# A product-key expert mixer: h in PSUM, two banks for the sums, more gathered rows beside the dot products

## What is computed

```python
q = (tb @ wq).reshape(PEER_BLOCK, PEER_HEADS, 2, PEER_QDIM // 2)
s = jnp.einsum('thcd,hcnd->thcn', q, keys)            # 2 x 128 scores a head
...                                                    # 16 best pairs a head: e, g
a = jax.nn.gelu(jnp.einsum('td,thkd->thk', tb, u_tab[e]), approximate=False)
return jnp.einsum('thk,thkd->td', (g * a), v_tab[e])
```

## Time and profile before

| | us |
|---|---|
| median of 3 runs (4033.55 to 4056.06) | 4041.88 |
| the profiled execution | 4036.62 |
| its span | 4034.8 |
| expert stage, first to last matmul | 2018.2 to 3948.3 |

### The profile page before, as it was taken

The page is one execution under the profiler, slowest core; times in us unless marked ns, Lnnn a source line. Parts: engine busy times, 40 slices in busy tenths (PEclk is TensorE's granted clock), DMA queues, the critical chain, the costliest instruction groups (busy, mean ns, idle before and its releaser), DMA issues. The chain is left out here.

```text
span 4034.8 us, 59078 instructions
## 1 busy us (share of the span) xinstructions
PE 3311.0 (82%) x20585; PEld 2890.3 (72%) x20585; DVE 2778.2 (69%) x5881; ACT 1357.6 (34%) x3190; POOL 1709.0 (42%) x1341
## 2 busy tenths in 40 slices
PE   6999688566686892666589999999999999999994
PEld 3677455211376792555489999999999999999993
DVE  3223676100231199999779998999999889999885
ACT  3010466000221111887633333333333333333331
POOL 1010000000212441888765665665565565565560
PEclk7999799777788996776699999999999999999997
DMA  6632546999422331787598998998988988898983
GB/s 232 221 124 74 172 148 212 357 412 406 161 72 77 99 115 42 200 240 205 141 329 318 330 325 303 326 331 311 326 319 314 334 316 314 320 322 307 328 300 148
DMA packets 389552, 1001.89 MB, mean 248 GB/s; under 512 B 187044, under 2 KB 232975, under 8 KB 325688
## 3 DMA queue, kind: packets, MB, share of 16 engines
q1 hardware_dynamic: 323768, 491.18, 35.9%
q0 software_dynamic: 62656, 469.86, 32.2%
q10 hardware_dynamic: 2944, 38.77, 2.6%
HBM read 914.75 MB, written 152.04 MB: 264 GB/s over the span
## 5 line engine op out<-in xcount | busy, mean ns | idle before, releaser
L2174 DVE CUSTOM_DVE_ANT_0 e_uv<-e_uv,e_h 128x1024 f32<-128x1024 f32 x416 | 721.7, 1735 | 73.8 <-DMA e_uv<-peer_uv,k_g_idx 73.1
L2243 POOL DMA_INDIRECT e_uv<-peer_uv,k_g_idx x416 | 521.1, 1253 | 540.4 <-DVE e_pY L2186 496.8
L1475 PE MATMUL e_po<-e_ph,e_vh 128*128 128x320 f32 x2048 | 646.3, 316 | 59.2 <-DVE k_OT L2218 55.1
L1475 PE MATMUL e_pa<-k_hi_d,e_uh 128*128 128x320 f32 x2048 | 638.4, 312 | 50.7 <-POOL e_ul L2234 37.5
L1476 PE MATMUL e_po<-e_pl,e_vh 128*128 128x320 f32 x2048 | 633.3, 309 | 0.0
L1477 PE MATMUL e_po<-e_ph,e_vl 128*128 128x320 f32 x2048 | 633.3, 309 | 0.0
L1477 PE MATMUL e_pa<-k_hi_d,e_ul 128*128 128x320 f32 x2048 | 633.2, 309 | 0.0
L1476 PE MATMUL e_pa<-k_lo_d,e_uh 128*128 128x320 f32 x2048 | 633.1, 309 | 0.0
L2186 DVE SCALAR_TENSOR_TENSOR e_pY<-e_uv,e_wts,e_pY 128x1024 f32<-128x1024 f32 x412 | 526.0, 1277 | 0.0
L1475 PEld LDWEIGHTS e_po<-e_ph,e_vh 128*128 128x128 f32 x2048 | 384.8, 188 | 83.7 <-DVE k_OT L2218 71.3
L1475 PEld LDWEIGHTS e_pa<-k_hi_d,e_uh 128*128 128x128 f32 x2048 | 384.8, 188 | 62.0 <-issue 46.0
(11 more groups left out here) (305 smaller groups left out, 5889.7 us busy)
## 6 DMA issues: line engine op xcount, KB each, us to landing
k_kv<-kv_pages SPq DMA_DIRECT2D x128, 512.0 KB, 7.0
s_kv<-kv_state SPq DMA_DIRECT2D x32, 2048.0 KB
e_v<-peer_uv SPq DMA_DIRECT2D x128, 512.0 KB
e_u<-peer_ut SPq DMA_DIRECT2D x126, 512.0 KB, 6.1
s_g<-r_G SPq DMA_DIRECT2D x10, 4096.0 KB
k_OT<-s_g SPq DMA_DIRECT2D x128, 320.0 KB
v_win_sample<-state_v_win POOLq DMA_DIRECT2D x28, 1168.0 KB, 10.0
k_win_sample<-state_k_win ACTq DMA_DIRECT2D x28, 1168.0 KB
```

The lines of the kernel that those rows point to most:

```text
L1475: nc.tensor.matmul(out, lhs_hi, rhs_hi, start=start, stop=False)
L2174: nc.vector.tensor_tensor_reduce(uv[:, r, 0:D], uv[:, r, 0:D], h[:], 1.0, 0.0, ALU.mult, ALU.add, dots[:, r:r + 1]).then_inc(row_dotted, 1)
L2243: nc.gpsimd.indirect_dma_start(uv[:, s % RING], None, io["peer_uv"], bass.IndirectOffsetOnAxis(ap=keep.g_idx[:, s:s + 1], axis=0),).then_i ...
```

## The change

1. `h` moves from SBUF to PSUM (two banks). To make room `po` has two banks instead of four (SUMS = 2).
2. `share` gives 12 of the 26 gather operations to the dots slots (1, 2, 1, 2, 1, 2, 1, 2) and 14 to the sums, none to tiles 0 and 8.
3. A dots slot first does the 16 products with `uh`, then the 8 with `ul`; PE waits for `uh` ahead of the slot and for `ul` ahead of its last 8. A sums tile does `vh` by `ph`, `vl` by `ph`, `vh` by `pl`, and waits for `vl` and `pl` only ahead of their products.
4. SP's loads stand in another order, each about where its buffer comes free; two `u` loads are ahead of the loop.
5. ACT does `split_u` of the slots 1 and 3 straight after the gelu, ahead of `ph`, and no more behind it.

```diff
-SUMS = 4
+SUMS = 2
...
-        h = sb("e_h", [P, D])
...
+        h = ctx.enter_context(nc.psum_tensor("e_h", [P, D], F32))
...
-            if slot >= DOTS:
-                first = NR - OUTS + slot - DOTS
-                return range(first, first + 1)
-            return range((NR - OUTS) * slot // DOTS, (NR - OUTS) * (slot + 1) // DOTS)
+            def before(x):
+                n = max(0, x - DOTS)
+                late = n - sum(KC * b < n for b in range(NBD))
+                return (NR - OUTS + NBD) * min(x, DOTS) // DOTS + late
+            return range(before(slot), before(slot + 1))
...
-                with sp.Fori(0, NK // 2 - 1) as i:
-                    for u in range(2):
-                        c = 2 * i + u
-                        sp.wait_ge(ul_done, c + 1)
-                        sp.dma_start(uu[:, u], uview[ds(c + 2, 1)].rearrange("a p k e -> (a p) k e")).then_inc(u_in[u], 16)
-                        sp.wait_ge(p_done, NBD * c + NBD + 2)
-                        sp.dma_start(G[:, u], row(io["s_g"], c + 2)).then_inc(g_in[u], 16)
-                        sp.wait_ge(vl_done, c + 1)
-                        sp.dma_start(vv[:, u], row(vview, c + 2)).then_inc(v_in[u], 16)
...
+                for c in (2, 3):
+                    load_u(0, c)
+                with sp.Fori(0, NQ - 1) as i:
+                    for load, c in ((load_v, 2), (load_g, 2), (load_u, 4), (load_v, 3), (load_g, 3), (load_u, 5), (load_g, 4),
+                                    (load_v, 4), (load_v, 5), (load_g, 5), (load_u, 6), (load_u, 7)):
+                        load(i, c)
...
-                    pe.wait_ge(ul_done, CQ * i + c + 1)
+                    pe.wait_ge(uh_done, CQ * i + c + 1)
...
                         for k in range(KC):
-                            x = split_product(nc, pa[:, m % 2, 0:WD], uh[:, c % 2, k], ul[:, c % 2, k],
-                                              keep.hi_d[:, k, cols], keep.lo_d[:, k, cols], k == 0, k == KC - 1)
+                            nc.tensor.matmul(pa[:, m % 2, 0:WD], uh[:, c % 2, k], keep.hi_d[:, k, cols], start=(k == 0), stop=False)
+                            nc.tensor.matmul(pa[:, m % 2, 0:WD], uh[:, c % 2, k], keep.lo_d[:, k, cols], start=False, stop=False)
+
+                        if b == 0:
+                            pe.wait_ge(ul_done, CQ * i + c + 1)
...
-                    pe.wait_ge(vl_done, CQ * i + CQ)
+                    pe.wait_ge(vh_done, CQ * i + CQ)
...
+                            if k == 0:
+                                pe.wait_ge(pl_done, DOTS * i + NBD * (CQ - 1) + b + 1)
...
                     nc.scalar.activation(pa[:, m % 2, 0:WD], pa[:, m % 2, 0:WD], ACT.Gelu).then_inc(gelu_done, 1)
+                    if b == 1 and c < 2:
+                        split_u(CQ * i + 2 + c)
...
-                        if m % NBD == 1 and m // NBD < 2:
-                            split_u(CQ * i + 2 + m // NBD)
```

More of the change, by code:

```diff
@@ L2038, in _, with load_u, load_g, load_v @@
                     sp.dma_start(G[:, u], io["s_g"][u]).then_inc(g_in[u], 16)
-                with sp.Fori(0, NK // 2 - 1) as i:
-                    for u in range(2):
-                        c = 2 * i + u
-                        sp.wait_ge(ul_done, c + 1)
-                        sp.dma_start(uu[:, u], uview[ds(c + 2, 1)].rearrange("a p k e -> (a p) k e")).then_inc(u_in[u], 16)
-                        sp.wait_ge(p_done, NBD * c + NBD + 2)
-                        sp.dma_start(G[:, u], row(io["s_g"], c + 2)).then_inc(g_in[u], 16)
-                        sp.wait_ge(vl_done, c + 1)
-                        sp.dma_start(vv[:, u], row(vview, c + 2)).then_inc(v_in[u], 16)
+                def load_u(i, c):
+                    sp.wait_ge(ul_done, CQ * i + c - 1)
+                    sp.dma_start(uu[:, c % 2], uview[ds(CQ * i + c, 1)].rearrange("a p k e -> (a p) k e")).then_inc(u_in[c % 2], 16)
+                def load_g(i, c):
+                    sp.wait_ge(p_done, NBD * (CQ * i + c - 1) + 2)
+                    sp.dma_start(G[:, c % 2], row(io["s_g"], CQ * i + c)).then_inc(g_in[c % 2], 16)
+                def load_v(i, c):
+                    sp.wait_ge(vl_done, CQ * i + c - 1)
+                    sp.dma_start(vv[:, c % 2], row(vview, CQ * i + c)).then_inc(v_in[c % 2], 16)
+                for c in (2, 3):
[4 more added lines that the diff above has]
+                        load(i, c)
+                for load, c in ((load_v, 2), (load_g, 2), (load_v, 3), (load_g, 3)):
+                    load(NQ - 1, c)
             @block.tensor
@@ L2061, in dot @@
                         for k in range(KC):
-                            x = split_product(nc, pa[:, m % 2, 0:WD], uh[:, c % 2, k], ul[:, c % 2, k],
-                                              keep.hi_d[:, k, cols], keep.lo_d[:, k, cols], k == 0, k == KC - 1)
+                            nc.tensor.matmul(pa[:, m % 2, 0:WD], uh[:, c % 2, k], keep.hi_d[:, k, cols], start=(k == 0), stop=False)
+                            nc.tensor.matmul(pa[:, m % 2, 0:WD], uh[:, c % 2, k], keep.lo_d[:, k, cols], start=False, stop=False)
+                        if b == 0:
+                            pe.wait_ge(ul_done, CQ * i + c + 1)
+                        for k in range(KC):
+                            x = nc.tensor.matmul(pa[:, m % 2, 0:WD], ul[:, c % 2, k], keep.hi_d[:, k, cols], start=False,
+                                                 stop=(k == KC - 1))
                         x.then_inc(dotted, 1)
                 def out(i):
-                    pe.wait_ge(vl_done, CQ * i + CQ)
+                    pe.wait_ge(vh_done, CQ * i + CQ)
                     for b in range(NBD):
                         cols = slice(b * WD, (b + 1) * WD)
-                        pe.wait_ge(pl_done, DOTS * i + NBD * (CQ - 2) + b + 1)
+                        pe.wait_ge(ph_done, DOTS * i + NBD * (CQ - 2) + b + 1)
                         for k in range(KC):
                             n = KC * b + k
+                            rows = slice(k * P, (k + 1) * P)
                             pe.wait_ge(added, OUTS * i + n + 1)
@@ L2075, in out @@
                                 if k == 0 and c == CQ - 1:
[L2076 to L2079, removed]
+                                    pe.wait_ge(ph_done, DOTS * i + NBD * (CQ - 1) + b + 1)
+                                nc.tensor.matmul(po[:, n % SUMS, 0:WD], vh[:, c, rows], ph[:, c, cols], start=(c == 0), stop=False)
+                            if n == 0:
+                                pe.wait_ge(vl_done, CQ * i + CQ)
+                            for c in range(CQ):
+                                nc.tensor.matmul(po[:, n % SUMS, 0:WD], vl[:, c, rows], ph[:, c, cols], start=False, stop=False)
+                            if k == 0:
+                                pe.wait_ge(pl_done, DOTS * i + NBD * (CQ - 1) + b + 1)
+                            for c in range(CQ):
+                                x = nc.tensor.matmul(po[:, n % SUMS, 0:WD], vh[:, c, rows], pl[:, c, cols], start=False,
+                                                     stop=(c == CQ - 1))
                             x.then_inc(summed, 1)
```

## The result

The changed kernel takes 4107.49 us (median of 4 runs, 4105.68 to 4110.20), the kernel before 4045.75 (4 runs, three of them those given ahead of the change; 4033.55 to 4056.06): 1.0154 times as long, 95% interval 1.0124 to 1.0185. I had said 3989, 3935 to 4040. The time lies outside, on the other side: the kernel is slower, where I had forecast a gain. Each ratio is uncertain by 0.2% to 0.6%, so such a difference is good to some 15 to 25 us.

What follows compares the result with a forecast made beforehand. PE was taken to bound the stage: 1806.3 us of matmuls, 8 in the first dots and 31 x (1.0 + 0.9 + 0.3) = 68 of waits give 1882 against 1930. With 50 us less in all, it forecast 3989 us, range 3935 to 4040.

Steps and rivals of the forecast that it cites:

- What bounds the kernel, and the 124 us to win: Whole stage: PE bounds it; 1930.3 us less 1806.3 of matmuls without a wait leaves 124 us to win.
- h in PSUM: DVE's `row_dot`: from 1.735 to 1.22 us, 214 us less DVE time, worth only what PE waited for it.
- Two banks: Sums tile 2: PE waits for addition 0 behind slot 7's gather operations, 0.9 us a round, taken as 1.0.
- lateness: Sums tile 2: a little lateness of the gather, with which the 0.9 us wait was taken as 1.0.
- POOL's written order: Dots: a stalled `pl` delays `vl` and the gather behind it, PE waits 2.9 us at tile 2; about 4072 us, chance 0.12.
- A gather behind `ul` in the sums: Sums tile 9: a gather issued after `ul` makes addition 7 late; PE waits 0 to 1.8 us a round, taken as 0.9.
- Twelve operations beside the dots: Dots slots: a stalled `pl` makes PE wait in some rounds, 0.3 us on average, bounds 0 and 1.
- Low products last, early split: Dots: PE's 15 us wait for `ul` goes to nothing, and PE begins 2.4 us earlier at the start.
- 0.5 twice a round: Dots: early `split_u` delays `ph` some 0.5 us, costing DVE that twice a round unless a gather operation hides it.
- Loads: New load order: gain inside the other terms; 380 GB/s in dots, 298 in sums, 334 a round, fits narrowly.
- The rule on a gather's time: Gathers: the skill's 4.4 us for 1.05 MB would remove the 0.9 for tile 6's `row_dot`; not taken, given rows of 6.3 to 8.85.
- The sum: Whole stage: 1806.3 + 8 + 31 x (1.0 + 0.9 + 0.3) = 68 gives 1882 us; kernel 3989.

Runs made afterwards that it cites:

- the two comparisons: Changed kernel with h back in SBUF, 60 us over the changed kernel; kernel before with h in PSUM and two banks, 33 us under two banks alone.
- with tile 2 mended: Changed kernel with eleven gather operations beside the dots, none at sums tile 0, one at each of tiles 1 to 15: 4033.47 us.
- the best kernel: Changed kernel with five gather buffers instead of four and eleven gather operations beside the dots: 3925.68 us, 0.9718 times before.
- the products and loads without h: Kernel before with low products last and the new load order alone (four banks, h in SBUF, old share, late split): 4075.88 us, 1.0094.

## Why the prediction was wrong, step by step

- *What bounds the kernel, and the 124 us to win*: right. The kernel with five buffers and eleven operations gains 111 us of span (4034.8 - 3923.4), 1930.3 - 1823.7 = 106.6 of it in the stage.
- *h in PSUM*: right in all sizes: `row_dot` 1.211 us (predicted 1.22), POOL's issues 0.953 without a tail (of the 1.76 us ones none is left). By the rule of the Trainium skill (SBUF — State Buffer, Who interferes with whom) a DVE instruction with at most one SBUF input does not contend with POOL; the trace agrees (maximum 1.225 in 416). But DVE time freed isn't PE time, as the prediction said: 218 us of it gave 33 to 60 us, by the two comparisons.
- *Two banks*: the step that failed. The term was 1.0 us a round for PE's wait at tile 2; it was 3.2, and 1.5 more for the lower clock. The chain in front of addition 0 (4.43 us) took both gathers at the end of the dots to be on time, but for 0.1 of "lateness". They were not: slot 6's `row_dot` waited 1.2 us and slot 7's 1.4, and the chain took 7.2. With five buffers, where neither is late, it takes 4.4 and PE waits 0.8, so all else in the chain was right. Nor is that the whole price of two banks: with the old share and loads they cost 44 us with h in PSUM, and no gather was late ahead of tile 2.
- *The rival "POOL's written order"* had most of the mechanism: it named the late gather behind `vl` of slot 4, priced the wait at tile 2 at 2.9 us and the round at 4.8, and gave 4072 us a chance of 0.12. It came nearest. In the round shown its first link is off by two slots: the `pl` that stalled (3.29 us at 3039.29) was slot 1's, and slot 3's took 0.49. That its time came within 35 us of the measured one is in part luck: the 0.9 at tile 9 wasn't there, and the lower clock was in none of its terms. I worked the chain with POOL's turns in it for this rival and not for the forecast.
- *The lower clock*: in no case of the prediction. Before, the longest waits for additions were 2.3 us and the clock stood at 1.00, so I took 0.147 us for every matmul. It cost 46 us by the trace; with PE kept busy the kernel was at 4057, 41 us lower.
- *A gather behind `ul` in the sums* (0.9 at tile 9): hidden in the changed kernel, where PE is late already; with tile 2 mended it came up one tile later, as 49 us at tile 10, 1.6 a round, of a size within the 0 to 1.8 that I gave it. That run has an operation at tile 8 that the changed kernel hasn't.
- *Twelve operations beside the dots*: 0.3 us a round at most, right; the dots are at 28.4. But their price is paid at tile 2: with ten operations beside the dots no gather was late there, with twelve two were. I had put no term there for the sixth gather.
- *Low products last, early split*: `ul` waits are gone, as predicted. That the early split can cost 47 us when h is in SBUF, or more when `u` is late, I had not seen; the "0.5 twice a round" left out that POOL's subtraction moves too, and what it then meets.
- *Loads*: I priced the new order at nothing beyond the terms above; with the early split it is worth 105 us. A round did need what I had added up, 334 GB/s, and the engines could give it: 338 went through the stage of the best kernel. The halves were the other way round: I had 380 in the dots and 298 in the sums, and that kernel has 283 in a dots half and 395 in its sums.
- *The rule on a gather's time*, from the Trainium skill (DMA: Bandwidth & Descriptors, Anatomy of one DMA): about 2.0 us and bytes at 436 GB/s, an estimate of 4.4 us. The trace doesn't agree under this load. The gather issued at 3055.27 was waited for until 3064.29, 9.0 us.
- *The sum*: predicted 31 x 2.2 = 68 us of waits and 8 in the first dots; measured 192 over the 1806: 101 at tile 2, 46 of slow matmuls behind it, 11 in the first dots, 34 of others. One slip beside it: the profiled execution lay 5 us under the median, and I added only some 3 for that.

Left open: why the products and loads without h lose in the sums (4075.88 us), how much the product order is worth by itself, and what issuing the gather ahead of `vl` would give with four buffers, which no run tried.

## What to carry to other kernels

Before taking buffers from the engine that bounds a kernel, ask for the longest single delay of its consumer, not its mean: two banks cover 3.5 us here, and a chain with two late transfers was 7.2. When an engine is freed and nothing is won, look at what it waits for next; here it was gathers from a ring that was one buffer too short, and the memory that the same change set free paid for it. A wait of the matrix engine can cost half as much again as it lasts.

## What the runs showed of the hardware

The granted clock of TensorE was 0.53 of 2.4 GHz, all but the 1.2 GHz level, for some 3 us after a wait of 3.7 us, in a stage where PE is otherwise busy; 101 us of waits brought 46 us of slow matmuls. Keeping PE at work with 20 useless matmuls in each wait took these away (clock 1.00, 1.0053 instead of 1.0154 times before). Waits of up to 1.8 us, 97 in the run with two banks alone, cost hardly more than themselves (clock 0.99 there).

A gather of 1 MB took at most 6.3 us from issue to use in a quiet stretch and 9.0 beside loads, in a stretch where the DMA engines were at a share of 0.97 and moved 368 GB/s. Over the whole stage they had room for more: 309 GB/s in the changed kernel, 338 with one buffer more.
